# The rows of summed squares as two float32r matmuls, and the mLSTM's columns of 1/rms taken out of the row

## The reference, cut to what matters

```python
def rms_norm(x, g):
    xf = x.astype(jnp.float32)
    y = xf * lax.rsqrt(jnp.mean(xf * xf, axis=-1, keepdims=True) + EPS)
    return (y * g.astype(jnp.float32)).astype(x.dtype)
```

## Time and profile before

| | |
|---|---|
| median of 3 runs | 1545.5 us (1544.36, 1545.5, 1545.63) |
| the profiled execution's own time | 1544.45 us |
| its span | 1542.7 us |
| PE busy | 1530.5 us, 12794 matmuls |
| DVE busy | 1045.6 us |
| ACT busy | 849.7 us |
| granted TensorE clock | 1.00 |

### The profile page before, as it was taken

The page is one execution under the profiler, slowest core; times in us unless marked ns, Lnnn a source line. Parts: engine busy times, 40 slices in busy tenths (PEclk is TensorE's granted clock), DMA queues, the critical chain, the costliest instruction groups (busy, mean ns, idle before and its releaser), DMA issues.

```text
span 1542.7 us, 34843 instructions
## 1 busy us (share of the span) xinstructions
PE 1530.5 (99%) x12794; PEld 1492.5 (97%) x12794; DVE 1045.6 (68%) x1766; ACT 849.7 (55%) x1302; POOL 122.5 (8%) x123
## 2 busy tenths in 40 slices
PE   9999999999999999999999999999999999999999
PEld 8899999988999999999999999999999998999999
DVE  7777765644876557666787766668576657787764
ACT  6776654546655445555445555556555547665543
POOL 1830000045000000000000000000000033200000
DMA  7156666554666665656665655656555972065564
GB/s 257 59 135 195 193 190 203 167 174 138 194 195 197 193 192 191 193 194 200 190 207 193 200 191 191 206 186 206 194 192 192 235 206 66 16 204 193 193 199 151
DMA packets 80783, 280.51 MB, mean 182 GB/s; under 512 B 8880, under 2 KB 12464, under 8 KB 80688
## 3 DMA queue, kind: packets, MB, share of 16 engines
q1 hardware_dynamic: 76512, 273.77, 55.8%
q10 hardware_dynamic: 4176, 5.38, 1.8%
HBM read 277.53 MB, written 1.57 MB: 181 GB/s over the span
## 4 chain that ended last, share of the span: by engine, by line
PE 94%; DVE 4%; ACT 1%; issue 1%; DMA 0%; SPq 0%; ACTq 0%; DVEq 0%
PE psum L1800 27%; PE psum L1804 27%; PE psum L1801 27%; PE psum L1948 2%; PE psum L1950 2%; PE psum L1949 2%; PE psum L2190 1%; PE psum L2239 1%; DVE w_lo L1067 1%; PE psum L2135 0%; DVE scratch L1664 0%; PE psum L2013 0%; PE psum L2223 0%; PE psum L2003 0%; DMA raw<-tiles 0%
## 5 line engine op out<-in xcount | busy, mean ns | idle before, releaser
L579 ACT ACTIVATE w_hi<-raw 128x1024 fp32r<-128x1024 f32 x515 | 544.1, 1059 | 474.8 <-PE psum L1804 437.2
L1067 DVE TENSOR_TENSOR w_lo<-raw,w_hi 128x1024 fp32r<-128x1024 f32 x480 | 587.2, 1224 | 251.8 <-ACT w_hi L579 251.5
L1800 PE MATMUL psum<-xs,w_hi 128*128 128x256 f32 x1904 | 528.8, 278 | 1.0 <-DVE w_lo L1729 0.8
L1801 PE MATMUL psum<-xs,w_hi 128*128 128x256 f32 x1904 | 526.0, 276 | 0.0
L1804 PE MATMUL psum<-xs,w_lo 128*128 128x256 f32 x1904 | 525.9, 276 | 0.0
L1800 PEld LDWEIGHTS psum<-xs,w_hi 128*128 128x128 f32 x1904 | 357.4, 188 | 2.1 <-DVE w_lo L1729 1.2
L1801 PEld LDWEIGHTS psum<-xs,w_hi 128*128 128x128 f32 x1904 | 357.4, 188 | 0.2
L1804 PEld LDWEIGHTS psum<-xs,w_lo 128*128 128x128 f32 x1904 | 357.3, 188 | 0.0
L1804 PE MATMUL psum<-hs,w_lo 128*128 128x256 f32 x1280 | 353.3, 276 | 0.0
L1800 PE MATMUL psum<-hs,w_hi 128*128 128x256 f32 x1280 | 353.3, 276 | 0.0
L1801 PE MATMUL psum<-hs,w_hi 128*128 128x256 f32 x1280 | 353.3, 276 | 0.0
(11 more groups left out here) (294 smaller groups left out, 1485.5 us busy)
## 6 DMA issues: line engine op xcount, KB each, us to landing
raw<-tiles SPq DMA_DIRECT2D x516, 512.0 KB, 4.2
bias<-bias_dram ACTq DMA_DIRECT2D x8, 256.0 KB, 6.1
w1c_all<-w1c_k ACTq DMA_DIRECT2D x4, 256.0 KB, 4.4
w1c_all<-w1c_v ACTq DMA_DIRECT2D x4, 256.0 KB, 6.1
y_out<-x SPq DMA_DIRECT2D x8, 128.0 KB, 3.4
con<-consts SPq DMA_DIRECT2D x1, 803.0 KB, 8.9
x<-x_in ACTq DMA_DIRECT2D x2, 256.0 KB, 4.8
raw<-tiles SPq DMA_DIRECT2D x2, 256.0 KB, 5.3
```

The source lines that it names most:

```text
L579: act.activation(slot_part(w_hi[s], t + RING * q if isinstance(q, int) else t), raw[s][:, :], ACT.Copy).then_inc(hi_ready, 1)
L1067: dve.tensor_tensor(slot_part(w_lo[s], t_), raw[s][:, :], hi_of(slot_part(w_hi[s], t_)), ALU.subtract).then_inc(lo_ready, 1)
L1800: pe.matmul(out, w_hi[s][:, c:c + P], x_hi, start=first, stop=False)
L1801: pe.matmul(out, w_hi[s][:, c:c + P], x_lo, start=False, stop=False)
```

## The change

The rows of all norms but `mix_0` are no longer summed by a float32 matmul. ACT writes a float32r copy of `ssq` into the first half of `ssq_parts`, DVE writes `ssq` minus this copy into the second half, and PE sums both by two float32r matmuls of ones (`ones_r`) into one PSUM row. `ssq_split` counts both writes. `ssq_parts` lies over the start of `scratch`, 16 columns in; `ones_r` is a float32r copy of `ones`, made by DVE at the start of the program, with a gap of 16 columns ahead of it; the gap ahead of `os` shrinks by 16.

In `two`, `sums` moves from ahead of the last chunk's six matmuls to behind them, and `odd_matmul` stays only for norms in `TO_COLUMNS`, which none of the stages with `odd` then has. `mix_1` leaves `TO_COLUMNS`: its two columns of 1/rms are taken out of one partition of the finished row `rb` by two float32 matmuls of one partition, in `turn_rows`, and copied by DVE in `columns`.

```diff
@@ -172,6 +172,8 @@
         w_lo = [sb(f"w_lo{s}", [P, TILE + 4 * ASIDE], F32R) for s in range(RING)]
         x = sb("x", [P, KD * S])
 
+        with nc.sbuf_tensor("ssq_parts", [P, 16 + 2 * S], F32R) as ssq_parts:
+            ssq_parts = ssq_parts[:, 16:]
         scratch = sb("scratch", [P, 12 * S])
         half, fsum, sq = ([scratch[:, (4 * j + s) * S:(4 * j + s + 1) * S] for s in range(4)] for j in range(3))
         sil = half[0:2]
@@ -179,6 +181,8 @@
         row = sb("row", [P, N_ROW])
         con = sb("con", [P, N_CONST])
         ones = sb("ones", [P, P])
+        sb("apart_r", [P, 16])
+        ones_r = sb("ones_r", [P, P], F32R)
         eps = sb("eps", [P, 1])
         std = sb("std", [P, 64])
         rstd = sb("rstd", [P, 64])
@@ -194,7 +198,7 @@
         kcT = sb("kcT", [P, G * NC])
         vc = sb("vc", [P, G * DH])
 
-        sb("apart", [P, 120])
+        sb("apart", [P, 104])
         with nc.sbuf_tensor("os", [P, KD * 2 * S], F32R) as os_:
             pass
         bias = sb("bias", [P, H * S])
@@ -232,7 +236,7 @@
         x_loaded = [sem(f"x_loaded{j}") for j in range(4)]
         n_gates = sem("n_gates")
         const_ready = sem("const_ready")
-        ssq_ready = sem("ssq_ready")
+        ssq_ready, ssq_split = sem("ssq_ready"), sem("ssq_split")
         stat_done, std_ready = sem("stat_done"), sem("std_ready")
         sq_ready = sem("sq_ready")
         xhi_ready, xs_ready = sem("xhi_ready"), sem("xs_ready")
@@ -415,7 +419,7 @@
         NORMS = ["mix_0", "cq", "ffn_0", "mix_1", "ffn_1", "pre_0", "mid_0", "post_0", "kvn", "mid_1", "post_1"]
         NEXT = dict(zip(RES, NORMS[2:]))
         TO_ROWS = [n for n in NORMS if n not in ("cq", "mid_1")]
-        TO_COLUMNS = ["mix_0", "cq", "mix_1", "kvn", "mid_1"]
+        TO_COLUMNS = ["mix_0", "cq", "kvn", "mid_1"]
         SUMS = [n for n in NORMS if n != "cq"]
         STAT0 = {n: j + 1 for j, n in enumerate(NORMS)}
         SSQ0 = {n: (KD + 1) * j for j, n in enumerate(SUMS)}
@@ -580,6 +584,9 @@
 
             def root(name):
 
+                if name in TO_ROWS and name != "mix_0":
+                    act.wait_ge(ssq_ready, SSQ0[name] + KD + 1)
+                    act.activation(ssq_parts[:, 0:S], ssq[:, :], ACT.Copy).then_inc(ssq_split, 1)
                 act.wait_ge(stat_done, STAT0[name])
                 if name in TO_ROWS:
                     act.activation(stdb[:, :], bank(RB, 0, S), ACT.Sqrt, bias=eps[:, 0:1], scale=1.0 / D).then_inc(std_ready, 1)
@@ -1071,6 +1078,10 @@
 
             def norm(name):
 
+                if name in TO_ROWS and name != "mix_0":
+                    hi, lo = ssq_parts[:, 0:S], ssq_parts[:, S:]
+                    dve.wait_ge(ssq_split, 2 * TO_ROWS.index(name) - 1)
+                    dve.tensor_tensor(lo, ssq[:, :], hi_of(hi), ALU.subtract).then_inc(ssq_split, 1)
                 dve.wait_ge(std_ready, STD0[name])
                 if name in TO_ROWS:
                     then(dve.reciprocal(rb[:, :], stdb[:, :]))
@@ -1421,6 +1432,7 @@
 
                 def columns():
                     dve.wait_ge(m_at, 1)
+                    then(dve.tensor_copy(rstd[:, 0:TB], bank(7, 2 * TB * MH, 2 * TB * MH + TB)))
                     dve.tensor_copy(m_col, bank(7, 0, 2 * TB * MH)).then_inc(m_cols, 1)
                     dve.wait_ge(m_cols, 1)
 
@@ -1729,6 +1741,8 @@
                 dve.tensor_tensor(w_lo[t][:, cols], raw[t][:, cols], hi_of(w_hi[t][:, cols]), ALU.subtract)\
                    .then_inc(half_lo if n == 0 else lo_ready, 1)
 
+            dve.wait_ge(const_ready, 1)
+            dve.tensor_copy(ones_r[:, :], ones[:, :])
             dve.wait_ge(vec_loaded, 16)
             for k in range(KD):
                 g = VEC["mix_0"] + k
@@ -1824,7 +1838,12 @@
                     if name == "mix_0":
                         pe.wait_ge(const_ready, 3)
                     if name in TO_ROWS:
-                        ins = pe.matmul(bank(RB, 0, S), ones[:, :], ssq[:, :], start=True, stop=True)
+                        if name == "mix_0":
+                            ins = pe.matmul(bank(RB, 0, S), ones[:, :], ssq[:, :], start=True, stop=True)
+                        else:
+                            pe.wait_ge(ssq_split, 2 * TO_ROWS.index(name))
+                            pe.matmul(bank(RB, 0, S), ones_r[:, :], ssq_parts[:, 0:S], start=True, stop=False)
+                            ins = pe.matmul(bank(RB, 0, S), ones_r[:, :], ssq_parts[:, S:], start=False, stop=True)
                     if name in TO_COLUMNS:
                         for tb in range(TB):
                             ins = pe.matmul(bank(STAT, tb, tb + 1), ssq[:, tb * P:(tb + 1) * P], ones[:, 0:1], start=True, stop=True)
@@ -1863,8 +1882,6 @@
                     pe.wait_ge(out_read, o0 + 1 - 3)
                     for k in range(KD):
                         pe.wait_ge(xs_ready, XS0[xs_name] + k + 1)
-                        if norm_ and k == KD - 1:
-                            sums(norm_)
                         for u in range(2):
                             ins = narrow_product((o0 + u) % 4, ((t0 + u) % RING, k * P), k, src, k == 0, k == KD - 1)
                             if k == KD - 1:
@@ -1876,8 +1893,9 @@
                 paired = norm_ is not None and outs > 1 and name != "dq"
                 if paired:
                     two()
-                if odd:
-                    odd_matmul()
+                    sums(norm_)
+                    if odd and norm_ in TO_COLUMNS:
+                        odd_matmul()
                 for u in range(2 if paired else 0, head):
                     one(u, 0, u == 0)
                     if u in between:
@@ -2064,7 +2082,10 @@
                     for n, src in enumerate((m_a, m_nm)):
                         for tb in range(TB):
                             col = (n * TB + tb) * MH
-                            ins = pe.transpose(bank(7, col, col + MH), src[:, tb * P:(tb + 1) * P], con[0:MH, CONST["ident"]:CONST["ident"] + MH])
+                            pe.transpose(bank(7, col, col + MH), src[:, tb * P:(tb + 1) * P], con[0:MH, CONST["ident"]:CONST["ident"] + MH])
+                    for tb in range(TB):
+                        col = 2 * TB * MH + tb
+                        ins = pe.matmul(bank(7, col, col + 1), rb[0:1, tb * P:(tb + 1) * P], ones[0:1, 0:1], start=True, stop=True)
                     ins.then_inc(m_at, 1)
 
                 def scores(h):
```

## The result

The kernel after takes 1551.76 us, the median of 20 runs, where the kernel before took 1544.47 us in 20 runs: ratio 1.0039 (95% interval 1.0026 to 1.0051), slower by 0.4%. The median hides two groups: 17 runs lie at 1551.4 to 1554.3 us, and three at 1541.42, 1541.44 and 1541.56 us. The time of the first group is the one that the prediction gave to its rival of a lost cadence (1551.6), that of the second is close to its forecast. The profiled execution, 1551.97 us with a span of 1550.2, is of the first group, so its trace shows what the 17 have in common.

What follows compares the result with a forecast made beforehand. PE bounds the kernel, busy 99% of the span. Gains of 2.7 + 0.2 + 0.35 = 3.25 us take the profiled 1544.45 to 1541.2 and the median of 1545.5 to 1542.2 us; range 1540.0 to 1552.0.

Steps and rivals of the forecast that it cites:

- rival of a lost cadence: A wait at `mid_0` ends slow and nothing restores PE's cadence before `kvn`: 9.4 us more, 1551.6 us; chance 0.19.
- the new chain to the row: PE's row waits for ACT's copy and DVE's subtraction; tightest at `mid_0`: ready 760.20 to 760.29, due 760.27, wait at most hundredths.
- Today the odd matmul ends each norm fast: In the kernel before, the odd matmul behind each norm's row leaves PE at its faster cadence, 113.3 ns a product.
- The sum: Gains of 2.7 us for six rows, 0.2 for `kvn` and 0.35 for `mix_1`: 3.25 us.
- a row alone: At six norms, float32 row and odd matmul (0.68 us) become two float32r matmuls (0.23): gain 0.45 us each.
- the rest of `mix_1`: Behind the eighth product's 0.90 us gain: fifth-tile wait 0.6, `turn_rows` 0.33, up to 0.48 from cadence; 0.35 left in all.
- The cover: Fifth tiles lose 0.9 us of lead; `cin`'s is ready at 765.74 and PE comes at 766.05, so it holds by 0.2.
- The row's own turn: The row itself turns the cadence slow over about 8500 products, `up_0` to `out_3`: 34 us, 1576; chance 0.05.
- `kvn`'s other state in `glu_2`: `kvn`'s new start makes 1200 products in `glu_2` and `out_2` slow: 4.8 us, 1547.0; chance 0.05.
- The eaten gain: Row matmuls cost like float32 passes, or `mgate` and fifth tiles wait: 1.5 to 2.8 us left, 1543.3; chance 0.16.
- the first rival: A wait at `mid_0` leaves PE slow until `kvn`: 1551.6 us, chance 0.19; void if one size has one gap.
- 1542.9 us without the cadence: The forecast under the skill's single gap for 256 columns, which drops 0.67 us of cadence in `mgate` from the sum.

Runs made afterwards that it cites:

- late_mid: The kernel after with a DVE memset of 256 columns ahead of the subtraction at `mid_0`; 1541.95 us, ratio 0.9991, two of ten runs at 1552.1 and 1556.2.
- rows_only: The kernel after with `mix_1`'s two columns kept as float32 column sums and the odd matmul behind them; 1553.13 us, ratio 1.0055.
- odd_mid: The kernel after with the odd matmul put back behind the row of `mid_0` alone; 1552.1 us, ratio 1.0048.
- odd_all: `early_add` with the odd matmul put back behind every norm's row; 1580.67 us in its one run.
- early_add: The kernel after with DVE's last addition to `ssq` in `residual` moved ahead of a tile's split; 1541.37 us, ratio 0.9981.
- no_gap: `early_add` with the two parts of the sum at the very start of `scratch`, without the 16-column gap; 1579.15 us, ratio 1.0223.
- early_gates: `early_add` with the split of `mgate`'s fifth tile moved between the two gate reads, the mask written behind it; 1540.51 us, ratio 0.9974.
- early_both: `early_add` with the split of `mgate`'s fifth tile moved to the head of `mlstm`; 1540.86 us, ratio 0.9973.
- cols_only: The kernel before with only `mix_1`'s columns taken from the row by one-partition matmuls, rows left float32; 1543.82 us, ratio 0.9994.

## Why the prediction was wrong, step by step

**The step that failed** is "the new chain to the row". The place was right, `mid_0` alone, and so were ACT's copy (0.42 against 0.41 us) and DVE's subtraction (0.42). The hand-over from DVE to PE was priced at 0.02 to 0.05 us, like those from ACT to DVE and from PE to ACT, and took 0.12. A load that waits for DVE alone began 0.05 us behind it in the kernel before (first fence: DVE ends at 14.48). The row's load has two waits in the program text, the old one for `ssq_ready` and the new one for `ssq_split` (L1844), and the new one stands in PE's queue as an instruction of its own, 0.05 us long at each of the eight rows (second fence). In `late_mid`, where the record of PE's last product ends at 758.75, the hand-over is 0.12 us as well (third fence: 758.81 to 758.93), so running matmuls are not what makes it long.

```profile
13.25 1.23 DVE L1067 TENSOR_TENSOR w_lo<-raw,w_hi 128x1024 fp32r<-128x1024 f32 x1 [0.33 <-ACT w_hi L579]
...
14.53 0.19 PEld L1800 LDWEIGHTS psum<-xs,w_hi 128*128 128x128 f32 x1 [0.27 <-DVE w_lo L1067]
```

```profile
L1844 PEldq EVENT_SEMAPHORE  x8: 51/51/51, 121.1 to 1372.0; - x8
```

```profile
758.39 0.42 DVE L1086 TENSOR_TENSOR ssq_parts<-ssq,ssq_parts 128x256 fp32r<-128x256 f32 x1
...
758.93 0.19 PEld L1847 LDWEIGHTS psum<-ssq_parts,ones_r 128*128 128x128 f32 x1 [0.38 <-issue]
```

That the separate wait makes the difference is argued from these rows; the change without its older wait, which the new one implies, was not run. The 0.12 us turned "ready at 760.20 to 760.29, due at 760.27" into 0.06 us late. Even with 0.05 the margin was about nothing, and the price of missing it was known: the forecast's range of readiness reached past the due time, so a chance of 0.19 for the lost cadence was too low. "Against: the wait is a few hundredths, and one restart of the two was fast" was the wrong reading of the earlier trace rows: two restarts give no odds, and in the runs a wait of hundredths ended slow in 17 of 20, the worst share of the four lengths seen. The eight runs of `rows_only` and `odd_mid`, which are as late at `mid_0`, were all slow.

**The price of this rival was right, by two errors that cancel.** 1551.6 us was forecast and 1551.76 measured. The difference of cadence is 4.4 to 4.5 ns by long windows, not 4.0, so at least 10.3 us instead of 9.4; and the level from which it counts is 1541.4, not 1542.2.

**"Today the odd matmul ends each norm fast"** holds in the order of the earlier trace rows and is no rule: `odd_mid` and `odd_all` show the same instruction leaving PE slow. The conclusion drawn from it, that nothing restores the cadence before `kvn`, came out as said.

**The sum was nearly right.** The three runs of the change with the cadence kept lie 3.0 us under the median before, where 3.25 were forecast; 1542.2 was too high for them because the median of three runs that it starts from lies 1.0 us over that of 20. From `early_add`'s timeline against that of before, at the second product of each stage's third tile: a lead of 0.43 us in `ffn_0`, 1.34 in `mgate` behind `mix_1`, 0.92 in `ffn_1`, then 0.46 more at each of `pre_0`, `mid_0` and `post_0`, and 2.96 in all at `post_1`. So a row alone gives 0.46 as priced (in `ffn_0` too, ahead of which PE was 0.03 late), `kvn` 0.2 as priced, and `mix_1` its 0.90 up to the eighth product. The term that was mis-sized is the rest of `mix_1`: from there to the row of `ffn_1` 0.88 us go back. The wait at the fifth tile was forecast at some 0.6 and took 0.63 with the late product behind it. The passes of `turn_rows` cost 0.45 us, not 0.33: they stand 0.11 us apart, more than the transposes that I took for their measure. And `mgate` went on slow behind its wait, where the sum had counted half of what a fast restart brings; there is no half. `mix_1` leaves 0.03 us in `early_add`, 0.12 in the change, both under the 0.35, and 0.70 in `late_mid`, where `mgate` restarted fast.

**The cover held.** PE does not wait at `cin`'s fifth tile, nor at any row but `mid_0`'s.

**The other rivals.** The row's own turn (1576) did not happen in the change and did in `no_gap` (1579), so "against: operands placed like the product's" was the right reason. `kvn`'s other state in `glu_2` (4.8 us) did not come with the change, whose `glu_2` is at 113.5 ns, but did in one run of `early_gates` (5.2). The eaten gain is refuted for the rows by their 0.46 us; at `mgate`, whose wait it names, little was left of the 0.35, as just told.

The Trainium skill, "TensorE: Matmul & The Clock Gate", section "Back-to-back issue gap", has one gap for 256 columns, an estimated 109 ns; it calls this the gap of an isolated matmul and has no figure for a stream of 256 columns. If the one gap held in a stream, the first rival was void; the windows of the change show 113.3 and 117.8 ns at one granted clock, so the measurement decides against that. The prediction's 1542.9 us without the cadence is 0.2 too high by its own terms: the 0.35 for `mix_1` counts on 48 products and on half of the other 119, 0.43 us of cadence and not 0.67.

## What to carry to other kernels

Where a change makes the engine that bounds the kernel wait for something new, work out for each place how long before it is due the operand is ready, with the hand-over as the instruction will have it (0.05 us here where the load itself waits, 0.12 where the wait is an instruction of its own); a margin of nothing is a miss. Ask then what a miss leaves behind, not only what it lasts: here 0.06 us of wait cost 10.3. The mend was an exchange of two instructions on an engine with time to spare, so look for the slack in the order of the feeding engine before giving a change up.

## What was unexpected of the hardware

- The cadence is a state that outlives its cause by over 2000 matmuls. At `early_both`'s fifth tile it turned with no more than a hundredth of a microsecond between the products to show for it, at `mgate` in the kernel after behind 0.53 us, and the same program falls on either side from run to run.
- A float32 matmul of 60 columns does not set the cadence to a known side, but one side is sure in these traces. In the thirteen profiles, counted instruction by instruction, it stands between products some 140 times: the 23 times that they came at 113 ns they went on at 118, without exception (`early_gates` above is one), and of the times that they came at 118 about two thirds went on at 113. The float32r row that leaves PE fast is therefore better off without it.
- A shift of the row's moving operands by 16 columns costs 37.8 us (1579.15 less 1541.37) with no wait in the trace. The Trainium skill, "SBUF — State Buffer", section "Who interferes with whom", gives PE a read port for the moving operand and another for the weight load, independent of each other, and lets only the port that VectorE and GpSimd share cause contention. This rule is about engines that meet and puts no price on an operand's place; this run has such a price, and what in the memory or in PE makes it no run shows.
- In some runs, one of `cols_only` among them, the granted clock falls for some microseconds in the sparse attention. In `late_mid`'s profiled run, columns as in the earlier trace rows:

```profile
1283.00:1287.00 4.00, 4.00 (x32) 3.61 (x31) 3.93 (x13) 1.56 (x4) 3.82 (x2) 1.00 0.39 134
...
1292.00:1296.00 4.00, 4.00 (x23) 2.75 (x22) 0.66 (x4) 1.43 (x5) 0.00 (x0) 0.50 0.02 4
```

0.50 is the level of 1.2 GHz. Ahead of the fall PE was marked busy throughout, with 32 matmuls in 4 us. The change's profiled run has 35 at these times, and no fall; what brings it these rows do not tell. Runs at 1552.9 to 1554.3 of the change are those with a mean clock under 1.00, and this is no part of what the change does.

Open stay what decides at a restart which cadence PE takes up, and what a float32 matmul and the operands' place have to do with it. The runs give odds for four lengths of wait at two norms, from 4 to 20 runs each, and no mechanism.
